# First layer's norm turned raw and divided behind the products; state-space buffers cleared by VectorE and GpSimd at the start

## The reference, cut to what matters

```python
hn = rmsnorm(x, even_norm)          # x * rsqrt(mean(x*x) + eps) * gain, per token
proj = hn @ even_w_in               # 1024 -> q 512 | k 128 | v 128 | u 512
q = rmsnorm(q per head, q_norm); k = rmsnorm(k per head, k_norm)
o_attn = swa_sink_attention(q, k, v, sinks)          # window 128
o_ssm  = s5_mixer(u, a, b, c, d, log_dt, w_glu, b_glu)   # state space, 64 states a group
mixed = concat([o_attn, o_ssm]) @ even_w_out; x = x + mixed
```

## Time and profile before

| | |
|---|---|
| three runs | 1575.22, 1573.0, 1575.1 us; median 1575.1 |
| profiled execution | 1573.85 us, its span 1572.0 us |
| granted TensorE clock, mean | 0.998 |
| busy over the span | TensorE 97%, VectorE 76%, ScalarE 55%, GpSimd 16% |
| memory | 264.65 MB moved, 168 GB/s |
| first layer's mixer, from the start | to about 120 us |
| its share by engine, 22.5 to 56.2 us | TensorE 32.58, VectorE 32.80, ScalarE 25.02 of 33.7 us |

### The profile page before, as it was taken

How to read it: one execution, slowest core, us unless ns; L and a number is a source line. 1 busy time by engine, 2 the same in 40 slices (tenths; PEclk the granted TensorE clock), 3 DMA queues, 4 the chain that set the end, 5 groups by cost and what they waited for, 6 DMA issues and landing times.

```text
span 1572.0 us, 30832 instructions
## 1 busy us (share of the span) xinstructions
PE 1532.6 (97%) x10479; PEld 1348.4 (86%) x10479; DVE 1201.6 (76%) x2342; ACT 860.8 (55%) x1316; POOL 248.7 (16%) x104
## 2 busy tenths in 40 slices
PE   7799999999999999999999999999999999999999
PEld 6778888888888888998899999988888888878887
DVE  7988888836688887775699852599999999975555
ACT  7755444568753446664555576555555444444543
POOL 2001000135200002000578757400000000000000
PEclk9999999999999999999999999999999999999999
DMA  6135555543465554433445555555554555555554
GB/s 228 55 100 183 187 186 192 182 148 121 146 207 194 190 187 160 159 117 114 161 157 184 178 177 183 190 166 170 172 173 161 174 173 173 173 174 193 194 193 154
DMA packets 72556, 264.65 MB, mean 168 GB/s; under 512 B 8080, under 2 KB 8336, under 8 KB 72112
## 3 DMA queue, kind: packets, MB, share of 16 engines
q1 hardware_dynamic: 71744, 261.00, 50.1%
q10 hardware_dynamic: 752, 2.83, 0.5%
HBM read 262.75 MB, written 1.05 MB: 168 GB/s over the span
## 4 chain that ended last, share of the span: by engine, by line
PE 86%; DVE 4%; ACT 2%; issue 1%; POOL 0%; ACTq 0%; DVEq 0%
PE ps L723 33%; PE ps L581 17%; PE ps L585 9%; PE ps L550 6%; PE ps L554 6%; PE ps L551 6%; PE ps L1195 2%; PE ps L639 1%; DVE arena L1812 1%; DVE w_lo L1812 1%; PE ps L1157 0%; ACT hT L1312 0%; PE ps L1007 0%; PE ps L677 0%; ACT w_hi L1286 0%
## 5 line engine op out<-in xcount | busy, mean ns | idle before, releaser
L1286 ACT ACTIVATE w_hi<-ring 128x1024 fp32r<-128x1024 f32 x489 | 515.3, 1057 | 355.3 <-PE ps L723 208.4
L1812 DVE TENSOR_TENSOR w_lo<-ring,w_hi 128x1024 fp32r<-128x1024 f32 x394 | 480.0, 1219 | 93.3 <-ACT w_hi L1286 79.1
L2708 POOL TENSOR_TENSOR w_lo<-ring,w_hi 128x1024 fp32r<-128x1024 f32 x95 | 240.1, 2538 | 750.3 <-DVE w_lo L1812 375.3
L581 PE MATMUL ps<-hT,w_hi 128*128 128x512 f32 x1184 | 298.4, 394 | 1.3 <-ACT w_hi L1286 1.3
L723 PE MATMUL ps<-w_hi,halves_hi 128*128 128x512 f32 x688 | 271.7, 395 | 0.6 <-DVE halves_lo L1812 0.6
L723 PE MATMUL ps<-w_hi,halves_lo 128*128 128x512 f32 x688 | 268.7, 391 | 0.0
L581 PEld LDWEIGHTS ps<-hT,w_hi 128*128 128x128 f32 x1184 | 215.1, 188 | 41.9 <-ACT w_hi L1286 1.7
L550 PE MATMUL ps<-hT,w_hi 128*128 128x256 f32 x968 | 242.4, 288 | 3.6 <-DVE hT L1848 2.7
L551 PE MATMUL ps<-hT,w_hi 128*128 128x256 f32 x968 | 237.8, 283 | 0.0
L550 PEld LDWEIGHTS ps<-hT,w_hi 128*128 128x128 f32 x968 | 185.3, 191 | 7.6 <-issue 4.8
L551 PEld LDWEIGHTS ps<-hT,w_hi 128*128 128x128 f32 x968 | 185.5, 192 | 0.1
(11 more groups left out here) (323 smaller groups left out, 1564.0 us busy)
## 6 DMA issues: line engine op xcount, KB each, us to landing
ring<-in_strips SPq DMA_DIRECT2D x489, 512.0 KB, 3.4
const<-in_const SPq DMA_DIRECT2D x1, 1352.0 KB, 11.7
x_s<-in_x SPq DMA_DIRECT2D x2, 512.0 KB, 4.6
arena<-in_rel ACTq DMA_DIRECT2D x1, 1024.0 KB, 4.8
arena<-in_keys ACTq DMA_DIRECT2D x1, 1024.0 KB, 6.1
out<-x_s SPq DMA_DIRECT2D x4, 256.0 KB, 2.2
arena<-in_ssm_bc SPq DMA_DIRECT2D x1, 512.0 KB, 6.8
arena<-in_ssm_b SPq DMA_DIRECT2D x1, 512.0 KB, 8.1
```

Of the source, the lines that this page charges most:

```text
L581: pe.matmul(bank, w[0][:, c * P:(c + 1) * P], hT[:, c].rearrange("p s t -> p (s t)"), start=c == 0, stop=False, skip_group_check=True)
L1286: sc.activation(w_hi[:, n % RING, :], ring[:, n % RING, :], ACT.Copy).then_inc(high_ready, 1)
L1812: return ve.tensor_tensor(o, a, b, op)
L2708: po.tensor_tensor(w_lo[:, n % RING, :], ring[:, n % RING, :], w_hi[:, n % RING, :].bitcast(F32), ALU.subtract).then_inc(low_ready, 1)
```

## The change

- The first norm joins those that scale behind the products (`SCALED_OUT`, bank 6). TensorE turns x raw as its halves land; it no longer waits for the root. ScalarE's squares and roots move behind the copies of k, q0 and q1; VectorE's inverse and diagonal (`scales(0)`) move behind `low(5)`.
- Behind `low(6)` VectorE takes the scale and scales the sums of squares of the heads; behind `low(7)`, `low(8)`, `low(9)` and `turns(8)` it writes u0 to u3 out of PSUM times `scale_row` (`u_out`), which ScalarE copied before. The inverse of the heads' roots is multiplied by `scale_row`. The copy of v takes the scale per token on ScalarE.
- On ScalarE the parameter table's Exp, Exp, Sin, Sin are taken apart and put around the parts; strips 0 and 1 are split earlier.
- On VectorE the second half of the angles (`decay_sines`) moves behind the parts.
- VectorE clears `e_F` first of all; GpSimd clears `e_X` first, then `e_K`, `e_h`, `e_m`, and then takes `low(0)` from VectorE.

```diff
-SCALED_OUT = [1, 2, 3, 4]
-SCALE_BANK = {1: 2, 2: 5, 3: 2, 4: 2}
+SCALED_OUT = [0, 1, 2, 3, 4]
+SCALE_BANK = {0: 6, 1: 2, 2: 5, 3: 2, 4: 2}
-SQ_MIX = 1
+SQ_MIX = 2
@@ TensorE
+                if i == 0:
+                    small_wait(pe, "first")
+                    for a in range(NT):
+                        small_wait(pe, "x%d" % a)
+                        for c in range(KC):
+                            mm = pe.transpose(norm_at(0, c)[:, a * P:(a + 1) * P], x_s[:, a, c * P:(c + 1) * P],
+                                              ident)
+                            if a == NT - 1:
+                                mm.then_inc(turned, 1)
+                    return
@@ in_matrices
+                    pe.wait_ge(scale_ready, 1)
@@ even, behind head_sums
+                widen_scale(0)
                 proj_fm(("even", "u", 0))
@@ ScalarE, norm
+                if i == 0:
+                    small_wait(sc, "param")
+                    sc.activation(e_p[:, 0, :], prm("log_dt"), ACT.Exp).then_inc(prm_act, 1)
+                    high_to(0)
+                    sc.wait_ge(prm_dve, 1)
+                    sc.activation(e_p[:, 3, :], e_p[:, 1, :], ACT.Exp).then_inc(prm_act, 1)
+                    parts()
+                    high_to(1)
+                    sc.wait_ge(prm_dve, 2)
+                    sc.activation(e_p[:, 9, :], e_p[:, 6, :], ACT.Sin).then_inc(prm_act, 1)
+                    sc.activation(e_p[:, 10, :], e_p[:, 7, :], ACT.Sin).then_inc(prm_act, 1)
+                    high_to(RING - 1)
+                    return
@@ ScalarE, even
-                for j in range(3):
+                for j in range(2):
                     out_and_square(("even", "q", j), j)
+                for a in range(NT):
+                    small_wait(sc, "x%d" % a)
+                    root(0, a)
+                out_and_square(("even", "q", 2), 2)
...
-                sc.wait_ge(sq_summed, 1)
-                sc.activation(e_rt[0:16, 0, :], ps[0:16, 1, 0:T], ACT.Sqrt, bias=k("eps")[0:16],
-                              scale=1.0 / HD).then_inc(rt_ready, 1)
-                out_u(0)
+                sc.wait_ge(sq_scaled, 1)
+                sc.activation(e_rt[0:16, 0, :], e_rt[0:16, 0, :], ACT.Sqrt,
+                              bias=k("eps")[0:16]).then_inc(rt_ready, 1)
+                u_split(0)
@@ VectorE, norm
+                if i == 0:
+                    ve.memset(e_F[:, :, :, :, :], 0.0).then_inc(zeroed, 1)
+                    small_wait(ve, "param")
+                    decay_angles()
+                    parts()
+                    decay_sines()
+                    return
@@ VectorE, even
-                for n in range(1, RING):
-                    low(n)
+                ve.wait_ge(low_ready, 1)
+                low(1)
                 small_wait(ve, "ssm")
                 ve.wait_ge(prm_act, 4)
+                low(2)
...
+                def u_out(j):
+                    ve.wait_ge(strip_done, AT[("even", "u", j)] + 1)
+                    ve.wait_ge(evac, 6 + j)
+                    m = 6 + j
+                    by_step = lambda a: a.rearrange("p (b s) -> p s b", s=LC)
+                    tt(e_u[:, j], by_step(ps[:, 4 + m % 2, 0:T]), by_step(scale_row), ALU.mult).then_inc(evac, 1)
                 low(5)
+                small_wait(ve, "first")
+                scales(0)
...
                 low(6)
+                take_scale(0)
+                scale_squares(1, e_rt[0:16, 0, :], 1)
...
                 low(7)
-                invert(1, e_rt[0:16, 0, :])
+                u_out(0)
+                invert(1, e_rt[0:16, 0, :], True)
...
                 low(8)
+                u_out(1)
...
                 low(9)
+                u_out(2)
                 turns(4)
...
                 turns(8)
+                u_out(3)
@@ GpSimd
+            po.memset(e_X[:, :, :, :, :], 0.0).then_inc(zeroed, 1)
             po.memset(e_K[:, :, :, :], 0.0).then_inc(zeroed, 1)
-            po.memset(e_F[:, :, :, :, :], 0.0).then_inc(zeroed, 1)
...
-            po.wait_ge(diag_ready, NT)
-            po.memset(e_X[:, :, :, :, :], 0.0).then_inc(zeroed, 1)
+            low(0)
```

More of the change, by code:

```diff
@@ L1297, in mix_split, with root @@
                     sc.activation(hT_hi[:, slots[j], :], mixT[:, j, :], ACT.Copy).then_inc(mix_high, 1)
+            def root(i, a):
+                ch.link(sc.activation(xn[:, a, :], x_s[:, a, :], ACT.Square, accum_out=stat[:, a:a + 1]))
+                sc.activation(stat[:, 2 + a:3 + a], stat[:, a:a + 1], ACT.Sqrt, bias=k("eps"),
+                              scale=1.0 / D).then_inc(roots, 1)
             def norm(i):
@@ L1303, in norm @@
                 first = 0 if i == 0 else AT[LASTS[i - 1]] + 1
-                ch.add(sc.activation(stat[:, 6:7], k("eps"), ACT.Sqrt))
+                ch.add(sc.activation(stat[:, 6:7], k("eps"), ACT.Sqrt if i else ACT.Exp))
                 if i:
@@ L1317, in norm @@
                         parts()
[L1318 to L1324, removed]
+                    sc.wait_ge(x_ready, 4 * (i - 1) + 2 * (a + 1))
+                    root(i, a)
                 if i == 3:
@@ L1331, in norm @@
                     small_load(sc, "keys", keys_s.rearrange("p a b -> p (a b)"), A["keys"])
[L1332 to L1340, removed]
                 if i not in SCALED_OUT:
@@ L1387, in out_and_square, with u_split @@
                     sc.activation(e_sq[:, c, :], ps[:, b, 0:T], ACT.Square).then_inc(evac, 1)
-                def out_u(j):
-                    out_of(("even", "u", j), e_u[:, j],
-                           lambda b: ps[:, b, 0:T].rearrange("p (b s) -> p s b", s=LC))
+                def u_split(j):
+                    high_to(AT[("even", "u", j)] + RING - 1)
+                    nproj[0] += 1
                 def exps(g):
@@ L1418, in even @@
                 high_to(AT[("even", "u", 2)])
-                sc.wait_ge(sq_summed, 1)
-                sc.activation(e_rt[0:16, 0, :], ps[0:16, 1, 0:T], ACT.Sqrt, bias=k("eps")[0:16],
-                              scale=1.0 / HD).then_inc(rt_ready, 1)
-                out_u(0)
+                sc.wait_ge(sq_scaled, 1)
+                sc.activation(e_rt[0:16, 0, :], e_rt[0:16, 0, :], ACT.Sqrt,
+                              bias=k("eps")[0:16]).then_inc(rt_ready, 1)
+                u_split(0)
                 sc.wait_ge(v_turned, 1)
-                sc.activation(e_v.rearrange("p a b -> p (a b)"), ps[:, 2, 0:T], ACT.Copy).then_inc(v_out, 1)
-                out_u(1)
+                for a in range(NT):
+                    ins = sc.activation(e_v[:, a, :], ps[:, 2, a * P:(a + 1) * P], ACT.Copy,
+                                        scale=stat[:, 4 + a:5 + a])
+                ins.then_inc(v_out, 1)
+                u_split(1)
                 for n in range(2 * (LC - 1)):
@@ L1433, in even @@
                               ACT.Copy).then_inc(decay_rows, 1)
-                out_u(3)
+                u_split(3)
                 out_wide_of(0)
@@ L1841, in norm @@
                     residual(i)
-                else:
-                    small_wait(ve, "first")
                 def parts():
@@ L1851, in parts, with scales @@
                                                 op1=ALU.subtract).then_inc(hT_low, 1)
+                if i == 0:
[5 more added lines that the diff above has]
+                    return
                 if i in SCALED_OUT:
                     parts()
+                scales(i)
+                if i not in SCALED_OUT:
+                    parts()
+            def scales(i):
                 for a in range(NT):
@@ L1859, in norm @@
                                      ALU.mult).then_inc(diag_ready, 1)
[L1860 to L1865, removed]
             def take_scale(i):
@@ L1885, in decay_angles, with decay_sines @@
                 ch.link(ve.scalar_tensor_tensor(out=p(5), in0=p(4), scalar=-C1, in1=p(2), op0=ALU.mult, op1=ALU.add))
-                ch.link(ve.scalar_tensor_tensor(out=p(5), in0=p(4), scalar=-C2, in1=p(5), op0=ALU.mult, op1=ALU.add))
+                ch.add(ve.scalar_tensor_tensor(out=p(5), in0=p(4), scalar=-C2, in1=p(5), op0=ALU.mult, op1=ALU.add))
+            def decay_sines():
+                p = lambda n: e_p[:, n, :]
+                ch.wait()
                 ch.add(ve.tensor_scalar(p(6), p(5), PI_LO, -PI_LO, ALU.min, ALU.max))
```

4 lines of the change are left out of this document (1 added, 3 removed).

## The result

The changed kernel takes 1577.29 us (median of 14 executions, 1576.13 to 1585.46); the kernel before, on the same chip, 1575.16 (14 executions, 1573.00 to 1576.76). The medians differ by 2.13 us (0.14%), where 1.8 us were forecast, to 1576.1. The ratio over all executions is 1.0025, 95% interval 1.0015 to 1.0034, which is the ratio of the means, 1578.97 and 1575.04: these differ by 3.9 us. The difference between the two figures is three executions at the top, 1584.70, 1585.18 and 1585.46; the other eleven have a mean of 1577.30. By the median the time lies inside the range given, 1572.3 to 1578.9, and among the cases that the prediction calls the same (up to 1578.25, chance 0.67); by the ratio it is slower by more than its 0.2% (chance 0.21). No case of the prediction has the three executions. Of the kernel before no execution in any job lies above 1577.11.

A forecast was written before the change was run, and what follows sets the result against it. VectorE's list of instructions was taken to bound the first block up to 105 us, then TensorE. A head gain of 2.25 us against 4.05 us added gave +1.8 us, hence 1576.1 us; eight in ten within 1572.3 to 1578.9.

The forecast's parts named there:

- the cases that the prediction calls the same: Whole kernel: a time from 1571.95 to 1578.25 us, about 0.2% or 3.15 us from no change; chance 0.67.
- The step that failed: First block, before the attention: TensorE waits for `low(7)` but loses nothing; +1.8 us is carried unchanged to the end.
- The head: Start of the first block: parts start 5.1 us earlier, but strip 3's landing limits the gain at `low(3)` to 2.25 us.
- The charge: Work added to VectorE behind `low(3)` in the first block: 4.05 us, ends 3.6 and 6.3.
- The base: Unchanged kernel's time to which the move was added: 1574.3 us, the mean of four executions.
- Rival 1: First block: VectorE's additions fit into links and idle times, charge under 1 us; faster, 1571.4 us; chance 0.14.
- Rival 3: Start: GpSimd and VectorE get in each other's way, `low(3)` done at 21.1; slower, +3.2 us, 1577.5; chance 0.11.
- Rival 4: Start: the head gives nothing, parts still start near 14 us; +4.05 + 0.5, 1578.8 us; chance 0.03.
- Rival 2: First projections: TensorE at half clock in k and q0, VectorE waits at `low(5)`; slower, +4.5 us, 1578.8; chance 0.12.

The follow-up runs named there:

- e1: The changed kernel with the large constants issued behind strip 3 instead of ahead of it; 1579.13 us, ratio 1.0027 against the kernel before.
- e2: The changed kernel with `u_out` reading in order, not by steps of four (regrouping of tokens left out); 1576.96 us, ratio 1.0010 against the kernel before.
- e8: The kernel before with four unused 128x512 products more on VectorE, where the changed kernel writes u; 1578.18 us, ratio 1.0030.
- e4: The kernel before with only the buffer clearing and `low(0)` moved as in the change; 1574.20 us, ratio 0.9995.
- e5: The changed kernel with 18 unused products on TensorE in its wait for `low(7)`; 1577.08 us, ratio 1.0023 against the kernel before.
- e9: The changed kernel with u copied raw by ScalarE and scaled by GpSimd instead of VectorE; 1577.26 us, ratio 1.0011 against the kernel before.
- e11: e8 with ten unused products on TensorE between the fourth and fifth head's scores; 1579.05 us, ratio 1.0025 against the kernel before.
- e3: The changed kernel with u copied by ScalarE and VectorE's `u_out` removed (scale of u left out); 1576.03 us, ratio 1.0008 against the kernel before.

## Where the prediction held, and where it failed

**The step that failed** is the one that took TensorE's waiting for VectorE as free: "TensorE then waits for `low(7)` where it ran through, and reaches the attention with nothing lost", with "carried unchanged" behind it. No term of the sum and no rival stands for the clock there. In its place the runs showed some 8 us in three of 14 executions, 1.7 us of the 3.9 by which the means differ. Beside it one term of the sum, `u_out`, was too small, 1.45 us for 2.13, and the sum was set on a base 0.86 us too low. What the prediction has right is the mechanism of the rest: in the trace of the changed kernel VectorE's list carries the head's gain and the additions, 2.38 us at the scores, up to x, 2.46.

**The head** went as forecast: parts at 8.74 (forecast 9.0), first projection product at 10.22 (10.4), `low(3)` at 19.05 (19.0) with VectorE idle before it, gain 2.28 us (2.25). e1 shows the stated cause, the landings.

**The charge** was mis-sized in one term. By their steps from start to start in the changed kernel: `scales` 0.79 us (forecast 0.9), `take_scale` 0.45 (0.45), `scale_squares` 0.79 (0.8), the product in `invert` 0.34 (0.45). `u_out` takes 0.51, 0.57, 0.53 and 0.52: 2.13 us, forecast 1.45, bounds 1.4 to 2.8. The estimate took the row read in order; e2 shows that the steps of four make the difference. The sum is 4.50 of the 4.66 found, for 4.05 forecast, and the scores are at 58.60, for 58.0. The ends of that sum were added up wrongly: its own bounds give 3.7 and 6.5 us, not 3.6 and 6.3.

**The base.** 1576.1 was built on the mean of the four times shown, 1574.3. The kernel's median over 14 executions is 1575.16, and in the later jobs 1575.07, 1574.95 and 1575.61. Of the 1.2 us between forecast and median, 0.86 are this choice and 0.33 the size of the move. The profiled execution of before, 1573.85, is one of its faster ones; e8 shows one thing that a slower one can have, the slow k, and no trace shows how often.

**Rival 1** (room for the additions) is false: 36.1 us are as full as 33.7 were. **Rival 3** (the clearings in each other's way) is false: VectorE's starts at 1.67 and ends at 5.14, under GpSimd's of the same size, which takes its 3.51 us as before. What does collide is GpSimd's reading: the 0.91 us of e4; in the changed kernel VectorE's angles are done at 8.1, before GpSimd's `low(0)` at 8.81. **Rival 4** is false.

**Rival 2** (TensorE cold in k) is right in its premise and wrong in its price. The 16 turns take 0.23 us each (3.68 / 16), and the first sixteen products of k follow each other by 0.21 us, from 10.22 to 13.56, where q0's take 0.12 from 14.84. The last eight of k are at full pace already, 1.06 us from 13.78 to q0's start, 0.13 each. The first sixteen cost little, because the parts that feed them come only every 0.40 us (3.23 / 8) for a pair that takes 0.43, and k ends at 14.84, not at 15.6. As said there, it would cost only if the low level outlived k, and here it did not. A low level can reach VectorE without outliving k: in e8, behind the head of the kernel before, it lasted to k's end (20.6, for 19.5), and `low(3)` came 1.15 us later. The granted clock column shows 1.00 for these first microseconds all the same, so at the head the step from product to product is the row to go by.

**What the prediction left out** is the clock at the other end. TensorE's waiting is free in 11 of 14 executions. In the other three it costs some 8 us: around its waits at the heads TensorE's clock falls to the 1.2 GHz level and stands there through 320 small products that VectorE needs next. The changed kernel's three were not profiled; that they are of this kind rests on the same step in time, on their mean clock (0.985 and 0.986, the others 0.991 to 0.995), and on e1, e5 and e8.

**A version that beats both** was not found. e4 has the lowest median, 1574.20, but its interval holds 1; the rest of the change costs more on VectorE than strip 3 lets the head give.

## What to carry to other kernels

When an engine is full for the next 80 us, an earlier start is worth only what it gains up to the next landing, and every factor that is moved behind the products is paid again by the full engine: list both before moving it, and price reads with steps apart from reads in order. An engine that waits for the full one is not free of charge either: look at whether its clock falls behind that wait and at what small work comes right behind it. Add up its waits before that work, and not only the last one. A profile shows one execution, so when a kernel has two groups of times, find the line that differs between a profile of each.

## What the runs showed of the hardware

- A product of 256 columns, one operand in PSUM and one in SBUF, takes 0.42 us read in order and 0.59 to 0.63 read by steps of four.
- Where the granted clock stood at 0.50 when `block_in` began, it stayed there through its 256 products of 32x64: 13.93 us, for 7.37 at 1.00 (e1, e2, e5, e8, e9). In e11 it rose from 0.50 to 1.00 behind ten products of 128x256.
- A stage ran at one level in one profile and at the other in the next, and that moves the waits behind it: in e9 the group of u3 ran at 1.00 (50 to 54 us) and came to its last eight products at 53.45, and the wait ahead of the first head is 1.86 us; in the changed kernel it fell to 0.50 (52 to 54 us), came to them at 54.46, and the wait is 0.40.
- The same fall elsewhere in the block costs less, and explains a part of the spread within the lower group. In e3's profile twelve turns took 2.82 us (1.53 before), and VectorE waited 1.79 us for ScalarE's parts, which come from them (at 88.67; no wait at that row before):

```profile
82.96 2.82 PE L896 MATMUL ps<-const,arena 128*128 128x128 f32 x12 [1.88 <-ACT arena L1466]
```

- Clearing 4096 columns takes VectorE 3.47 us and GpSimd 3.51, at the same time; GpSimd took 3.51 alone too, and no row shows VectorE alone. A GpSimd instruction that reads holds VectorE's two-operand steps in SBUF, even of 16 columns (0.91 us for a pair, 0.26 alone).
